# Seven products for eight in the full down projections of a two-layer encoder on one core

## What is computed

```python
for l in range(DEPTH):
    ...
    x = x + mixed @ w_out[l]
    h = _rmsnorm(x, g_ffn[l])
    z = _dwconv_centred(h @ w_up[l], conv_w[l], conv_b[l])
    z_gate, z_val = jnp.split(z, [D_FF], axis=-1)
    x = x + (jax.nn.silu(z_gate) * z_val) @ w_down[l]
return _rmsnorm(x, g_final)
```

## Time and profile before

| | us |
|---|---|
| time, median of 3 runs | 1104.07 |
| lowest and highest of them | 1103.85, 1104.14 |
| span of the profiled execution | 1102.4 |
| TensorE busy in it | 1092.6 |
| VectorE, ScalarE, GpSimd busy | 531.0, 484.7, 464.8 |

### The profile page before, as it was taken

One profiled execution on the slowest core, in us unless ns is written; L12 is line 12 of the kernel. 1 busy time (PEld: TensorE's weight loads), 2 busy tenths in 40 slices (PEclk: granted clock), 3 DMA queues, 4 the chain that ended last, 5 costly groups with the idle time before them and its releaser, 6 DMA issues.

```text
span 1102.4 us, 16315 instructions
## 1 busy us (share of the span) xinstructions
PE 1092.6 (99%) x5328; PEld 905.8 (82%) x5328; DVE 531.0 (48%) x816; ACT 484.7 (44%) x656; POOL 464.8 (42%) x202
## 2 busy tenths in 40 slices
PE   9999999999999999999999999999999999999997
...
PEclk9999999999999999999999999999999999999999
...
GB/s 301 93 96 78 68 76 105 78 109 100 96 95 94 97 96 95 96 96 97 180 97 81 91 63 74 95 77 96 115 95 76 115 96 95 79 117 91 96 77 78
DMA packets 33607, 108.79 MB, mean 99 GB/s; under 512 B 3984, under 2 KB 6800, under 8 KB 33552
## 3 DMA queue, kind: packets, MB, share of 16 engines
...
## 4 chain that ended last, share of the span: by engine, by line
PE 97%; DVE 1%; DMA 1%; ACT 0%; POOL 0%; SPq 0%; issue 0%; DVEq 0%
PE acc L1044 28%; PE acc L1045 28%; PE acc L1046 28%; PE acc L1170 3%; PE acc L1171 3%; PE acc L1172 3%; PE side L1140 1%; PE side L1258 1%; PE side L1242 1%; DMA x<-xT 1%; PE side L1248 1%; PE side L1221 1%; DVE arena L1019 1%; PE side L1201 1%; PE acc L1132 0%; PE acc L1121 0%
## 5 line engine op out<-in xcount | busy, mean ns | idle before, releaser
L339 POOL TENSOR_TENSOR w_lo<-w_raw,w_hi 128x1024 fp32r<-128x1024 f32 x188 | 453.4, 2416 | 600.6 <-ACT w_hi L348 600.6
L1044 PE MATMUL acc<-xg_hi,w_hi 128*128 128x512 f32 x864 | 338.8, 392 | 0.0
L1045 PE MATMUL acc<-xg_lo,w_hi 128*128 128x512 f32 x864 | 336.3, 389 | 0.0
L1046 PE MATMUL acc<-xg_hi,w_lo 128*128 128x512 f32 x864 | 336.2, 389 | 0.0
L348 ACT ACTIVATE w_hi<-w_raw 128x1024 fp32r<-128x1024 f32 x190 | 200.0, 1057 | 255.2 <-PE acc L1046 219.2
L1044 PEld LDWEIGHTS acc<-xg_hi,w_hi 128*128 128x128 f32 x864 | 162.2, 188 | 35.8 <-issue 2.0
L1046 PEld LDWEIGHTS acc<-xg_hi,w_lo 128*128 128x128 f32 x864 | 162.2, 188 | 33.9
L1045 PEld LDWEIGHTS acc<-xg_lo,w_hi 128*128 128x128 f32 x864 | 162.2, 188 | 33.5 <-issue 0.5
L1044 PE MATMUL acc<-feat_hi,w_hi 128*128 128x512 f32 (+1 forms) x492 | 188.9, 384 | 0.0
L1045 PE MATMUL acc<-feat_lo,w_hi 128*128 128x512 f32 (+1 forms) x492 | 188.8, 384 | 0.0
L1046 PE MATMUL acc<-feat_hi,w_lo 128*128 128x512 f32 (+1 forms) x492 | 188.8, 384 | 0.0
...
## 6 DMA issues: line engine op xcount, KB each, us to landing
w_raw<-slabs SPq DMA_DIRECT2D x190, 512.0 KB, 3.3
...
ln_sb<-ln_gb SPq DMA_DIRECT2D x2, 512.0 KB, 7.7
...
x<-xT ACTq DMA_DIRECT2D x1, 512.0 KB, 7.2
...
```

The lines of the kernel that those rows point to most:

```text
L339: pool.tensor_tensor(w_lo[:, w], w_raw[:, w], w_hi[:, w].bitcast(F32), ALU.subtract).then_inc(lo_done, 1)
L1044: pe.matmul(out, wh, ah, start=first, stop=False)
L1045: pe.matmul(out, wh, al, start=False, stop=False)
L1046: return pe.matmul(out, wl, ah, start=False, stop=last)
```

## The change

Both groups of four down products of each full part are computed by Winograd's form of Strassen's scheme. The four output tiles and the eight feature tiles are taken as a 2 by 2 by 2 block product: weights in four slabs of a new cut (`quad_major`: even or odd feature tiles, first or second tile of each pair of outputs), features as even and odd tiles, each in two halves of 256 tokens. Seven unit products take the place of eight. A unit is 4 pairs of tiles, 2 output tiles and 3 matmuls each of 256 columns: 24 matmuls of 256 columns for one slab of weights.

- VectorE makes four weight sums of 128 by 1024 for each group: `sum_s1`, `sum_s2`, `sum_s4`, and raw slab 0 minus slab 1 in place. The three other units take slabs as loaded.
- VectorE makes four feature sums (`t_raw`) of 128 by 256 for each pair of features, ScalarE their high parts, VectorE their low parts (`up_pair` for `up_quad`).
- ScalarE makes seven high parts and GpSimd seven low parts for each group, before four each.
- A bank holds two output tiles of 256 tokens; VectorE adds banks to x seven times a group, some of them part results that the next unit goes on from. TensorE's program for the down products is written out for both groups with waits on `lo_sum`, `lo_done`, `t_ready`, `feat_ready` and `unit_added`.
- GpSimd's loop over all slabs becomes stretches of the old loop with the seven low parts of a group between them.

```diff
-            with pool.Fori(1, DEPTH * NS // RING) as q:
-                for j in range(RING):
-                    w = slice(j * SLAB, (j + 1) * SLAB)
-                    pool.wait_ge(hi_done, q * RING + (j + 1))
-                    pool.tensor_tensor(w_lo[:, w], w_raw[:, w], w_hi[:, w].bitcast(F32),
-                                       ALU.subtract).then_inc(lo_done, 1)
...
+            def low_quad(L, part, g):
+                n, slab = quad_at(L, part, g)
+                pool.wait_ge(hi_sum, 3 * n + 1)
+                low(0, raw(0)).then_inc(lo_sum, 1)
+                pool.wait_ge(hi_sum, 3 * n + 2)
+                low(1, sum_s1).then_inc(lo_sum, 1)
+                pool.wait_ge(hi_done, L * NS + slab + 1)
+                pool.wait_ge(sum_done, 4 * n + 4)
+                low(2, sum_s2[:, :]).then_inc(lo_done, 1)
+                pool.wait_ge(hi_sum, 3 * n + 3)
+                low(3, raw(2)).then_inc(lo_sum, 1)
+                pool.wait_ge(hi_done, L * NS + slab + 2)
+                low(0, raw(1)).then_inc(lo_done, 1)
+                pool.wait_ge(hi_done, L * NS + slab + 3)
+                low(1, sum_s4).then_inc(lo_done, 1)
+                pool.wait_ge(hi_done, L * NS + slab + 4)
+                low(2, raw(3)).then_inc(lo_done, 1)
...
+                def up_pair(slab, tile, stage, even, odd, t_of, split):
...
+                            act.wait_ge(y_ready, (f + b) * 2 + v + 1)
+                            on_its_own(act)
+                            act.activation(z[j], y[j], ACT.Identity,
+                                           scale=conv_sb[:, bass.ds(coef + 1, 1)],
+                                           bias=conv_sb[:, bass.ds(coef + 3, 1)]).then_inc(centre_done, 1)
+                            split(j)
+                            if j == 2:
+                                act.wait_ge(t_done, stage * 2 + 1)
+                                on_its_own(act)
+                                act.activation(even(H), t_raw[:, 0:H], ACT.Copy).then_inc(t_hi_done, 1)
+                            if v == 0:
+                                act.wait_ge(taps_done, (f + b) * 4 + 2)
...
+                    act.wait_ge(t_done, stage * 2 + 2)
+                    on_its_own(act)
+                    act.activation(odd, gated[1], ACT.Copy).then_inc(feat_hi_done, 1)
+                    act.activation(t_of, t_raw[:, H:4 * H], ACT.Copy).then_inc(t_hi_done, 1)
...
+                def down_quads(part):
+                    n, slab = quad_at(L, part, 0)
+                    last_units(n, slab)
+                    act.wait_ge(unit_done, 7 * n + 5)
+                    first_units(n + 1, slab + RING, 0)
+                    first_units(n + 1, slab + RING, 1)
+                    act.wait_ge(unit_done, 7 * n + 6)
+                    first_units(n + 1, slab + RING, 3)
+                    act.wait_ge(unit_done, 7 * n + 7)
+                    first_units(n + 1, slab + RING, 2)
+                    last_units(n + 1, slab + RING)
+                    for j in range(RING):
+                        act.wait_ge(unit_done, 7 * n + (12, 13, 14, 14)[j])
+                        raw_at(j, slab + 2 * RING)
+                        split_hi(j)
...
+                    t1, t2, t3, t4 = (t_raw[:, i * H:(i + 1) * H] for i in range(4))
+                    scale(0)
+                    taps(0, 0)
+                    if sums is not None:
+                        sums(1)
+                        sums(2)
+                    scale(1)
+                    taps(0, 1)
+                    gate(0)
+                    if sums is not None:
+                        sums(4)
+                        sums(3)
+                    scale(2)
+                    dve.wait_ge(feat_hi_done, L * NF + tile + (KT + 1))
+                    dve.tensor_tensor(lo(0, H), gated[0][:, 0:H], hi(0, H).bitcast(F32),
+                                      ALU.subtract).then_inc(feat_ready, 1)
+                    dve.wait_ge(even_copied, stage + 1)
+                    dve.tensor_tensor(t1, gated[0][:, H:S], even_copy, ALU.subtract).then_inc(t_done, 1)
+                    taps(1, 0)
+                    dve.wait_ge(t_hi_done, stage * 2 + 1)
+                    dve.tensor_tensor(lo(H, H), t1, hi(H, H).bitcast(F32), ALU.subtract).then_inc(t_ready, 1)
+                    scale(3)
+                    taps(1, 1)
+                    gate(1)
+                    dve.wait_ge(gated_done, f + 2)
+                    dve.tensor_tensor(t2, gated[1][:, H:S], t1, ALU.subtract).then_inc(t2_done, 1)
+                    dve.wait_ge(t2_done, stage + 1)
+                    dve.tensor_tensor(t3, t2, gated[0][:, 0:H], ALU.subtract)
+                    dve.tensor_tensor(t4, gated[1][:, 0:H], t2, ALU.subtract).then_inc(t_done, 1)
+                    if added is not None:
+                        added()
+                    dve.wait_ge(feat_hi_done, L * NF + tile + (KT + 2))
+                    dve.tensor_tensor(lo(S, S), gated[1], hi(S, S).bitcast(F32), ALU.subtract).then_inc(feat_ready, 1)
+                    dve.wait_ge(t_hi_done, stage * 2 + 2)
+                    dve.tensor_tensor(t_lo[:, t_at], t_raw[:, H:4 * H], t_hi[:, t_at].bitcast(F32),
+                                      ALU.subtract).then_inc(t_ready, 1)
...
+                        if which == 1:
+                            loaded(1)
+                            loaded(3)
+                            if g:
+                                dve.wait_ge(lo_sum, 3 * n - 1)
+                            dve.tensor_tensor(sum_s1, raw(1), raw(3), ALU.add).then_inc(sum_done, 1)
+                        elif which == 2:
+                            loaded(0)
...
+                            dve.tensor_tensor(sum_s4, raw(2), sum_s2[:, :], ALU.subtract).then_inc(sum_done, 1)
+                        else:
+                            dve.tensor_tensor(raw(1), raw(0), raw(1), ALU.subtract).then_inc(sum_done, 1)
...
                 with dve.Fori(0, FULL_PARTS) as part:
-                    for half, hi, lo in ((0, feat_hi, feat_lo), (1, feat2_hi, feat2_lo)):
-                        with dve.Fori(0, 2) as q:
-                            up_quad(part * PART + q * RING + (N_FFN + half * 8), part * KT + q * 2 + half * 4,
-                                    lambda b: hi[:, bass.ds(q * (2 * S) + b * S, S)],
-                                    lambda b: lo[:, bass.ds(q * (2 * S) + b * S, S)])
-                    with dve.Fori(0, KT // RING) as q:
-                        for j in range(RING):
-                            add_to_x(L * NS + part * PART + q * RING + (N_FFN + 2 * KT + j), q * RING + j, j)
...
+                    stage_of(1, feat2_hi, feat2_lo, 1, sums_of(part, 0),
+                             lambda: add_unit(0, 0, 0, 0, 7 * n + 1, unit_added))
+                    add_unit(0, 1, 1, 1, 7 * n + 2, unit_added)
+                    add_unit(0, 0, 1, 0, 7 * n + 3, unit_added)
+                    add_unit(0, 0, 1, 1, 7 * n + 4, x_done, 3 * n + 3)
+                    add_unit(0, 1, 1, 0, 7 * n + 5, x_done, 3 * n + 2)
+                    make = sums_of(part, 1)
+                    make(1)
+                    add_unit(0, 0, 0, 2, 7 * n + 6, x_done, 3 * n + 1)
+                    make(2)
+                    make(4)
+                    make(3)
+                    add_unit(0, 1, 0, 0, 7 * n + 7, x_done)
...
+                def unit(bank, slot_of, pairs, moving, first):
+
+                    for k in pairs:
+                        for r in range(2):
+                            a = slot_of * SLAB + r * (SLAB // 2) + k * P
+                            xh, xl = moving(k)
+                            out = acc[bank][:, r * H:(r + 1) * H]
+                            pe.matmul(out, w_hi[:, a:a + P], xh, start=(first and k == 0 and r == 0), stop=False,
+                                      skip_group_check=True)
+                            pe.matmul(out, w_hi[:, a:a + P], xl, start=False, stop=False, skip_group_check=True)
+                            last = pe.matmul(out, w_lo[:, a:a + P], xh, start=False, stop=(k == KP - 1),
+                                             skip_group_check=True)
+                    return last
...
+                    pe.wait_ge(lo_sum, 3 * n + 1)
+                    pe.wait_ge(y_ready, ys + 1)
+                    pe.wait_ge(feat_ready, feats + KT - 1)
+                    unit(0, 0, every_pair, b11, True).then_inc(unit_done, 1)
+
+                    pe.wait_ge(lo_sum, 3 * n + 2)
+                    pe.wait_ge(y_ready, ys + 2)
+                    pe.wait_ge(t_ready, stages + 2 * KP - 1)
+                    unit(1, 1, every_pair, t1, True).then_inc(unit_done, 1)
+
+                    pe.wait_ge(lo_sum, 3 * n + 3)
+                    pe.wait_ge(y_ready, ys + 3)
+                    unit(2, 3, range(0, 2), b21, True)
...
+                    pe.wait_ge(lo_done, L * NS + slab + 1 + RING)
+                    pe.wait_ge(unit_added, 3 * n + 1)
```

(33 more changed lines are left out.)

196 lines of the change are left out of this document (183 added, 13 removed).

## The result

| | us |
|---|---|
| before, median of 4 runs, one more than above (lowest, highest) | 1104.07 (1103.85, 1104.14) |
| after, median of 4 runs (lowest, highest) | 1152.76 (1150.05, 1154.68) |
| ratio, with its 95% interval | 1.044 (1.042 to 1.046) |
| forecast, with its range | 1142 (1129 to 1161) |
| span of the profiled execution, before and after | 1102.4 and 1152.0 |

The changed kernel is slower by 48.7 us. The profiled execution took 1153.92 us itself, 1.2 above the median; its span is 49.6 above that of before, and this is what the traces have to explain.

The account below looks back on a forecast made before the run. TensorE, busy 99% of the span, was taken as the bound. Each full part would go from 43.5 to 40.3 + 12.9 = 53.2 us, +38.8 over four parts from 1104.07: 1142.9, say 1142, range 1129 to 1161.

Parts of the forecast that it names:

- The pace and the saving: TensorE's down products: 256-column matmuls start 0.120 us apart, so a full part's work falls from 43.5 to 40.3 us.
- The exclusion: A VectorE sum of two SBUF operands and a GpSimd low part never overlap; weight sums would average near 2.3 us.
- The rival without it: Weight sums and low parts run together; only the ScalarE and GpSimd order costs, +3.1 us a part, 1116 us; chance 0.07.
- Step 1: Up pair before the last: VectorE is free 13.3 us before the last up product ends, and not 16.1.
- Step 3: Second unit of the first down group waits for VectorE's low part of the first feature sum: stall 1.6 us.
- Steps 4 to 6: Later down units wait for low parts: stalls 2.1 and 3.6 us in the first group, 0.1, 0.6, 1.9 in the second.
- the forecast's own sum of 1142.9: Whole kernel: four full parts at +9.7 us each, +38.8 us in all, added to 1104.07 us.
- the forecast's own case: Whole kernel slowed by the stalls in the down products, clock at its upper level: 1132 to 1150 us, chance 0.60.
- the clock rival: TensorE's clock falls at the down products' waits, costing 2.6 to 5 us a part: 1153 to 1163 us; chance 0.23.
- Largest wait ahead of b22: TensorE's largest single wait, near 3.6 us, stands before this first-group down unit, ended by GpSimd's low part.
- TensorE idle 12 to 13 us in each stretch: The profile would show TensorE idle this long in each stretch of two down groups and nowhere else.

Follow-up runs that it names:

- c2: Against the kernel before: only the second group of each full part takes seven unit products, with weight sums made during the first group and VectorE's low parts deferred; 1097.33 us.
- e1: Changed kernel with each weight sum's second SBUF operand replaced by one spread PSUM column, so the output is not the reference's; 1134.11 us.
- e4: Changed kernel with VectorE's low parts of a pair's odd feature and sums moved behind the next pair's first scaling, last pair unchanged; 1133.22 us.
- e2: Changed kernel with spare matmuls of 256 columns into free banks where TensorE would wait in the down products; 1150.64 us.
- c1: Changed kernel with ScalarE's two high parts earlier, VectorE's low parts deferred, and the third and fourth weight sums behind the first unit's feature sum; 1118.04 us.

## Why the forecast was right, and where its value was off

**The pace and the saving: right.** Starts of 256 columns are 0.120 us apart (291.79 to 291.91 above), 336 of them 40.3 us. c2 shows the saving by itself, 1.6 us a group where the forecast had 3.2 a part.

**The exclusion: right.** The sums' mean is 1.91 us over the 32 ((20.7 + 16.3 + 14.4 + 9.7) / 32), for the 2.3 I named, and 1.21 where nothing was in the way, for the 1.22 estimated. GpSimd's low parts have a mean of 2.43 us for 2.42 before, so the exclusion falls on VectorE (22 us over the 32 sums) far more than on GpSimd (4 us over 212 low parts). e1 took it away from the weight sums and gained 18.6 us. The rival without it would have been 1116 with the other steps as forecast. That e1 took 1134.1 is for the most part b11's wait, 13.1 us over the four parts, which that rival had at nothing; the rest is t1's wait, which e1 left (3.3), and time at the lower clock.

**Step 1, the last pair's start: this step failed.** It had VectorE free for the last pair's first scaling 13.3 us ahead of the last up product's end, with nothing carried over from the pairs before ("makes it up by the second tile"). VectorE's timeline in the first and second part, the fourth scaling of the pair before and the first of the last pair:

```profile
260.09 0.69 DVE L1095 TENSOR_TENSOR side<-acc,rstdT 128x512 f32<-128x512 f32 x1
...
268.09 0.69 DVE L1095 TENSOR_TENSOR side<-acc,rstdT 128x512 f32<-128x512 f32 x1
...
400.50 0.69 DVE L1095 TENSOR_TENSOR side<-acc,rstdT 128x512 f32<-128x512 f32 x1
...
408.50 0.69 DVE L1095 TENSOR_TENSOR side<-acc,rstdT 128x512 f32<-128x512 f32 x1
```

With ends of the last up product at 277.21 and 420.94, the first scaling of the last pair comes at -9.1 and -12.4, so 4.2 and 0.9 us behind the forecast (and 7.0 behind the up product it scales, which ends at -16.3, plus a hand-over of 0.2); b11's delay is 6.75 and 3.5 for 2.6, later by 4.15 and 0.9. The chain from this first scaling to b11 is as forecast (15.9 us both), so b11's whole error is in where it starts. It is carried. In the first part of a layer the chain begins late:

```profile
196.51 3.35 DVE L827 RECIPROCAL rstdT<-rstdT 128x512 f32<-128x512 f32 x1 [2.33 <-ACT rstdT L431]
200.48 0.70 DVE L1095 TENSOR_TENSOR side<-acc,rstdT 128x512 f32<-128x512 f32 x1 [0.62 <-DVE rstdT L827]
```

The first up product had ended at 195.6 (16 of 5.44 us end at 277.21), so the first scaling is 4.7 us late by its own norm. The kernel before had the same row, with its first scaling 0.6 us behind it:

```profile
196.97 3.35 DVE L695 RECIPROCAL rstdT<-rstdT 128x512 f32<-128x512 f32 x1 [2.32 <-ACT rstdT L379]
```

It cost nothing there, since VectorE had caught up by the part's last tile, where it waited 1.86 us for TensorE. Now each border of pairs adds 2.6 to 2.8, as forecast, and within a pair only 1.6 to 2.8 us are made up, 0 to 1.6 a tile. At its fourth scaling VectorE is late by 3.1, 4.3 and 4.4 us in the first three pairs of the first part (the last of these is 260.09 above, against an end of 255.45 and the hand-over of 0.2), and by 0, 1.1 and 1.1 in the second part (400.50 against 399.4). So the lateness wasn't made up but carried to the end. e4, which takes just 1.65 us of work off each border, takes the wait away in both kinds of part; that the RECIPROCAL alone makes the difference between them is read from the trace and wasn't tried.

**Step 3, t1: right in size, and covered.** 1.57 in e2 and 1.51 in e4 for 1.6. In the changed kernel b11 ran at half clock for longer than that wait.

**Steps 4 to 6: right.** At full clock (e2) 2.08 for 2.1, 3.26 for 3.6, and 0.37 and 1.75 for 0.6 and 1.9 in the second group. The sum of the steps behind b11 is 9.0 for 9.9 forecast, with restarts 9.7 for 10.3. So a second part would have been 53.46 us at full clock, for 53.2 forecast: b11's 0.9 more and the others' 0.6 less.

**The clock: the rival came true in kind and not in size.** The forecast had it at 1.00 with 0.60 and the fall, at 1153 to 1163, with 0.23. It fell, and cost 4.0 us in the profiled execution, where the rival had 2.6 to 5 a part. Its argument against a fall, that no wait is longer than the work round it by much, was no safe one: in c1 the clock fell behind a wait of 1.9 us. Against the forecast's own sum of 1142.9: both first parts 3.6 more each, the clock 4.0, both second parts 0.26 more each, so 1154.6 for the profiled execution's 1153.92. That this lies at the foot of the rival's range (the median, 1152.76, is just below it) is the first parts' doing more than the clock's, 7.2 us against 4.0. And the median is 2.8 above 1150, the upper end of the forecast's own case: it lies inside the stated range only because that range took in the clock rival, and what carried it there was mostly step 1's backlog, which no rival had. That part is luck.

**"Largest wait ahead of b22"** was wrong: it is b11's, 6.6 (b22's is 3.1). "TensorE idle 12 to 13 us in each stretch": the first window has 56.66 - 43.91 = 12.75, which looks right for a wrong reason, since TensorE's slow stretch counts as busy. Against the 40.3 us of its work it lost 16.3.
